# Last two slabs of the output projection taken token tile by token tile, and the first two tiles of the norm before the channel mixer turned by transposes

## What is computed

```python
mix = jnp.concatenate([h_ml.reshape(B, T, ML_WIDTH), h_cm.reshape(B, T, CM_WIDTH)], axis=-1)
x = x + gt1 * (mix @ w_out)
h2 = rmsnorm(x, g_norm2) * (1 + sc2) + sh2
a, bb = jnp.split(h2 @ w_gate_up, 2, axis=-1)
x = x + gt2 * ((jax.nn.silu(a) * bb) @ w_down)
```

## Time and profile of the kernel before

| | us |
|---|---|
| median of 3 executions | 2568.75 |
| lowest, highest | 2564.78, 2570.92 |
| the profiled execution, its own time | 2567.24 |
| its span, first to last instruction | 2565.6 |
| PE busy in it | 2484.3 (97%) |
| DVE busy | 1203.4 (47%) |
| ACT busy | 846.5 (33%) |

### The profile page before, as it was taken

One profiled execution on the slowest core, in us unless ns is written; L12 is line 12 of the kernel. 1 busy time (PEld: TensorE's weight loads), 2 busy tenths in 40 slices (PEclk: granted clock), 3 DMA queues, 4 the chain that ended last, 5 costly groups with the idle time before them and its releaser, 6 DMA issues.

```text
span 2565.6 us, 32860 instructions
## 1 busy us (share of the span) xinstructions
PE 2484.3 (97%) x12360; PEld 1996.8 (78%) x12360; DVE 1203.4 (47%) x1759; ACT 846.5 (33%) x1148; POOL 161.5 (6%) x130
## 2 busy tenths in 40 slices
PE   4999999999999999999999999999989999999997
PEld 2678777788888788888888888888857877777775
DVE  4557544434337554444336554444365754333323
ACT  2243322233244243333244243333244323333211
POOL 0022000000004000000003000000002300000000
PEclk8999999999999999999999999999989999999998
DMA  7732545332342243332242233332333222222222
GB/s 270 247 102 84 173 149 157 92 100 99 99 125 67 94 123 94 94 101 94 89 140 74 95 115 94 95 98 91 103 118 107 79 73 75 82 81 81 85 89 75
DMA packets 358691, 275.93 MB, mean 108 GB/s; under 512 B 10992, under 2 KB 302356, under 8 KB 358567
## 3 DMA queue, kind: packets, MB, share of 16 engines
q1 hardware_dynamic: 330500, 224.57, 29.4%
q10 hardware_dynamic: 24116, 34.95, 4.0%
q0 software_dynamic: 3968, 14.95, 1.5%
HBM read 263.49 MB, written 10.96 MB: 107 GB/s over the span
## 4 chain that ended last, share of the span: by engine, by line
PE 85%; DVE 8%; issue 2%; DMA 2%; ACT 2%; ACTq 1%; POOL 0%; DVEq 0%; POOLq 0%; SPq 0%
PE banks L1751 17%; PE banks L1752 17%; PE banks L1753 17%; PE banks L1804 8%; PE banks L1806 8%; PE banks L1805 8%; PE banks L1765 1%; PE banks L1629 1%; DVE w_lo L1263 1%; DMA raw<-in_w_in_dram 1%; ACT w_hi L784 1%; PE banks L1775 1%; PE banks L1879 1%; DVE hT_lo L1269 1%; DVE x L1591 1%
## 5 line engine op out<-in xcount | busy, mean ns | idle before, releaser
L1751 PE MATMUL banks<-hT_hi,w_lo 128*128 128x512 f32 x2176 | 868.2, 399 | 11.0 <-DVE w_lo L1263 8.5
L1752 PE MATMUL banks<-hT_lo,w_hi 128*128 128x512 f32 x2176 | 853.3, 392 | 0.0
L1753 PE MATMUL banks<-hT_hi,w_hi 128*128 128x512 f32 x2176 | 852.4, 392 | 0.0
L1263 DVE TENSOR_TENSOR w_lo<-raw,w_hi 128x1024 fp32r<-128x1024 f32 x392 | 480.4, 1226 | 646.9 <-ACT w_hi L784 635.7
L784 ACT ACTIVATE w_hi<-raw 128x1024 fp32r<-128x1024 f32 x392 | 412.6, 1053 | 470.8 <-PE banks L1806 442.7
L1751 PEld LDWEIGHTS banks<-hT_hi,w_lo 128*128 128x128 f32 x2176 | 412.1, 189 | 115.9 <-issue 15.5
L1753 PEld LDWEIGHTS banks<-hT_hi,w_hi 128*128 128x128 f32 x2176 | 411.6, 189 | 88.2
L1752 PEld LDWEIGHTS banks<-hT_lo,w_hi 128*128 128x128 f32 x2176 | 412.2, 189 | 81.3
L1804 PE MATMUL banks<-w_lo,act_hi 128*128 128x512 f32 x704 | 277.2, 394 | 0.0
L1806 PE MATMUL banks<-w_hi,act_hi 128*128 128x512 f32 x704 | 274.2, 390 | 0.0
L1805 PE MATMUL banks<-w_hi,act_lo 128*128 128x512 f32 x704 | 274.1, 389 | 0.0
(11 more groups left out here) (332 smaller groups left out, 1880.4 us busy)
## 6 DMA issues: line engine op xcount, KB each, us to landing
raw<-in_w_gate_up_dram SPq DMA_DIRECT2D x176, 512.0 KB, 3.7
raw<-in_w_in_dram SPq DMA_DIRECT2D x96, 512.0 KB, 3.8
raw<-in_w_down_dram SPq DMA_DIRECT2D x88, 512.0 KB, 3.7
ada_stage<-in_w_ada_dram ACTq DMA_DIRECT2D x8, 2048.0 KB
raw<-in_w_out_dram SPq DMA_DIRECT2D x32, 512.0 KB, 3.7
in_stage<-in_w_in_dram ACTq DMA_DIRECT2D x6, 2048.0 KB
stage<-in_w_ada_dram SPq DMA_DIRECT2D x4, 2048.0 KB
x_sb<-in_x_prompt_dram POOLq DMA_DIRECT2D x4, 2048.0 KB, 9.0
```

The costliest lines, as they stand in the source:

```text
L1263: ve.tensor_tensor(w_lo[:, s % 2], raw[:, s % 2], w_hi[:, s % 2].bitcast(F32), ALU.subtract).then_inc(lo_done.sem, 1)
L1751: mm(out, w_lo[:, slot, k, :], rhs_hi[:, r, :], start=start and n == 0, stop=False)
L1752: mm(out, w_hi[:, slot, k, :], rhs_lo[:, r, :], start=False, stop=False)
L1753: ins = mm(out, w_hi[:, slot, k, :], rhs_hi[:, r, :], start=False, stop=stop and last)
```

## The change

The last two output slabs are no longer taken one after the other. When slab 6 is due PE waits for it, skips it, waits for slab 7 as well, and then does for each token tile the six matmuls of slab 6 and the six of slab 7. `out_tiles` on DVE now takes the mean square of a tile directly behind its residual sum, and the factor's use one tile later. For the first two tiles (ROW_TILES = 2) DVE and ACT multiply the rows themselves by the factor into `xn` (left half DVE, right half ACT), and PE turns them with transposes; for tiles 2 and 3 the diagonals stay, now for all eight pieces of a tile in one go. ACT's split of S_UP moves to the point in front of the squares of tile 3; in the last block DVE's copy to `s_ev` moves in front of the mean of tile 3, and the piece whose PSUM bank it frees is turned late.

```diff
+ROW_TILES = 2
@@ ACT
+            def scale_tile_right(blk, i):
+                act.wait_ge(rs.sem, rs.at(blk, i + 1))
+                act.activation(xn[:, KT // 2:KT, i, :], x1[:, i, BLK:D].rearrange("p (k e) -> p k e", e=P),
+                               ACT.Copy, scale=rrt[:, i:i + 1]).then_inc(up_right.sem, 1)
...
-                for n in range(1, N_OUT + 1):
+                for n in range(1, N_OUT):
                     split_hi(blk, S_OUT + n)
...
                 for i in range(TT):
+                    if i == TT - 1:
+                        split_hi(blk, S_UP)
                     act.wait_ge(zadd.sem, zadd.at(blk, TT + i + 1))
                     squares(blk, 0, x1, BLK, D, 1, rows=(i,))
+                    if 0 < i <= ROW_TILES:
+                        scale_tile_right(blk, i - 1)
@@ DVE
+            def scale_tile_left(blk, i):
+                ve.wait_ge(rs.sem, rs.at(blk, i + 1))
+                ve.tensor_scalar(xn[:, 0:KT // 2, i, :], x1[:, i, 0:BLK].rearrange("p (k e) -> p k e", e=P),
+                                 rrt[:, i:i + 1], None, ALU.mult).then_inc(up_left.sem, 1)
...
-                    if j == 1 and i > 0:
-                        tile_mean(blk, TT, i - 1)
-                    if j == 1 and i > 1:
-                        tile_diagonal(blk, i - 2)
+                    if j == 0:
+                        continue
+                    if i > 0:
+                        if i <= ROW_TILES:
+                            scale_tile_left(blk, i - 1)
+                        else:
+                            tile_diagonal(blk, i - 1)
+                    if last and i == TT - 1:
+                        ve.tensor_copy(s_ev[:, :], N2[:, :]).then_inc(sem("s_evict"), 1)
+                    tile_mean(blk, TT, i)
...
-                tile_mean(blk, TT, TT - 1)
-                for i in (TT - 2, TT - 1):
-                    tile_diagonal(blk, i)
-                if last:
-                    ve.tensor_copy(s_ev[:, :], N2[:, :]).then_inc(sem("s_evict"), 1)
+                tile_diagonal(blk, TT - 1)
                 split_lo(blk, S_UP)
@@ PE, up_norm
+                        if i < ROW_TILES:
+                            ins = pe.transpose(out, xn[:, k, i, :], ident[:, :])
+                        else:
+                            ins = mm(out, x1[:, i, k * P:(k + 1) * P], dg[:, i, :], start=True, stop=True)
...
+                held = UP_NORM_BANK.index(N2)
+                left, right = range(KT // 2), [k for k in range(KT // 2, KT) if not last or k != held]
+                for i in range(ROW_TILES):
+                    pe.wait_ge(up_left.sem, up_left.at(blk, i + 1))
+                    turn(i, left)
+                for i in range(ROW_TILES):
+                    pe.wait_ge(up_right.sem, up_right.at(blk, i + 1))
+                    turn(i, right)
+                for i in range(ROW_TILES, TT):
+                    pe.wait_ge(dg_tile.sem, dg_tile.at(blk, i - ROW_TILES + 1))
+                    if last and i == TT - 1:
                         pe.wait_ge(sem("s_evict"), 1)
+                        for r in range(TT - 1):
+                            turn(r, (held,))
+                    turn(i, [*left, *right] if last and i < TT - 1 else range(KT))
@@ PE, output slabs
                     slab_ready(blk, S_OUT + n)
+                    if n == N_OUT - 2:
+                        continue
                     for i in range(TT):
...
+                        if n == N_OUT - 1:
+                            ins = tile_product(OUT_BANK[i][:, :], (n - 1) % 2, mix_hi, mix_lo, 2 * (q - 1), i,
+                                               False, False)
+                            if i == TT - 1:
+                                ins.then_inc(slab_used.sem, 1)
                         ins = tile_product(OUT_BANK[i][:, :], n % 2, mix_hi, mix_lo, 2 * q, i, q == 0,
                                            q == OUT_Q - 1, before_k=ready)
```

More of the change, by code:

```diff
@@ L327, in hybrid_step @@
         MEANS = {-1: 0, 0: TT, 1: TT + 1, 2: TT + 2}
-        dg_tile = signal("dg_tile", TT)
+        dg_tile = signal("dg_tile", TT - ROW_TILES)
+        up_left = signal("up_left", ROW_TILES)
+        up_right = signal("up_right", ROW_TILES)
         left_scaled = signal("left_scaled", TT)
@@ L1403, in tile_ready, with out_tiles @@
                     ve.wait_ge(slab_used.sem, slab_used.at(blk, end))
-            def out_tiles(blk, j):
+            def out_tiles(blk, j, last):
                 cols = slice(j * BLK, (j + 1) * BLK)
@@ L1521, in ve_block @@
                     if n % OUT_Q == 0:
-                        out_tiles(blk, n // OUT_Q - 1)
-                tile_mean(blk, TT, TT - 1)
-                for i in (TT - 2, TT - 1):
-                    tile_diagonal(blk, i)
-                if last:
-                    ve.tensor_copy(s_ev[:, :], N2[:, :]).then_inc(sem("s_evict"), 1)
+                        out_tiles(blk, n // OUT_Q - 1, last)
+                tile_diagonal(blk, TT - 1)
                 split_lo(blk, S_UP)
@@ L1826, in turn @@
                             pe.wait_ge(out_read.sem, out_read.at(blk, TT + {0: 1, 5: 2, 6: 3, 7: 4}[k]))
-                        ins = mm(UP_NORM_BANK[k][:, i * P:(i + 1) * P], x1[:, i, k * P:(k + 1) * P], dg[:, i, :],
-                                 start=True, stop=True)
+                        out = UP_NORM_BANK[k][:, i * P:(i + 1) * P]
+                        if i < ROW_TILES:
+                            ins = pe.transpose(out, xn[:, k, i, :], ident[:, :])
+                        else:
+                            ins = mm(out, x1[:, i, k * P:(k + 1) * P], dg[:, i, :], start=True, stop=True)
                         if i == TT - 1:
                             ins.then_inc(trx.sem, 1)
[L1832 to L1836, removed]
+                held = UP_NORM_BANK.index(N2)
[9 more added lines that the diff above has]
+                    if last and i == TT - 1:
                         pe.wait_ge(sem("s_evict"), 1)
-                    for i in range(TT):
-                        turn(i, (k,))
+                        for r in range(TT - 1):
+                            turn(r, (held,))
+                    turn(i, [*left, *right] if last and i < TT - 1 else range(KT))
             def norm_out(blk, ks):
```

## The result

| | us |
|---|---|
| median of the kernel before | 2566.13 (2562.49 to 2570.92, 6 runs) |
| median of the changed kernel | 2579.51 (2577.84 to 2583.02, 6 runs) |
| ratio after to before, 95% interval | 1.0053 (1.0039 to 1.0066) |
| difference | +13.4 (+10.0 to +16.9) |
| profiled execution of after, its own time | 2578.35 (span 2576.7) |

The change makes the kernel slower by half a per cent. The two differences agree once one sees that the profiled execution of after lies 1.2 under its median, and that of before 1.1 over its median.

What follows compares the result with a forecast made beforehand. PE was busy 97%, held before the up slabs by DVE's chain. 2.57 + 0.11 - 0.58 = 2.10 us per block, 6.3 for three, +0.15 last: +6.4; clock +4.4; +10.8 on 2567.9 gives 2578.7 us, range 2571 to 2586.

Steps and rivals of the forecast that it cites:

- The wait: PE ahead of slab 6: waits for slab 7's split, 2.57 us per block in three blocks, 1.97 in the last.
- The 0.11 of the first matmul: PE's first matmul after the new wait takes 0.50 us instead of 0.39, adding 0.11 per block.
- DVE's backlog: Tiles 2.72 us apart let DVE keep up; tile 3's gate product starts 0.20 after its end, 0.58 us gained per block.
- The margins: DVE's means and ACT's work between tiles fit with 0.2 to 0.3 us to spare, costed at nothing.
- The chain behind tile 3: From tile 3's gate product to the last diagonal: unchanged at 3.22 us.
- The turns: PE's passes behind the last diagonal: 16 instead of 40, 2.8 us less work, costed at nothing because DVE's pieces don't wait.
- the turns were the bound: Rival: passes behind the last diagonal set the end, so a gain of 4.2 us, 2563.7 us; chance 0.06.
- The last block's sum: Last block: 1.97 wait less 0.64 samples' product, 0.58 backlog and 0.60 copy to `s_ev`, +0.15 us.
- The clock: Behind the new wait the granted clock falls in two of three blocks at 2.2 us each, +4.4 us.
- 1.58 us is harmless: PE's clock: an idle stretch of 1.58 us left it at 1.00, whereas one of 3.05 ended below.
- The transposes as a rival: Rival: transposes don't count as work for PE's clock, up to 1.8 us per block more, 2584.0 us; chance 0.10.
- What moved along: SP's slab loads and POOL's load of the next block's rows stay or shift with the chain; nothing gained or lost.

Runs made afterwards that it cites:

- e1: The kernel before with one wait more: PE waits for slab 7's split ahead of slab 6, old order kept; 2579.43 us against 2565.04, ratio 1.0057.
- e3: The changed kernel with slab 7 in a third slot of its own, so PE need not wait for its split; 2565.75 us against 2565.04, ratio 1.0001.
- e6: The changed kernel with slabs 6 and 7 one after the other again; scaled rows, transposes and new DVE/ACT order stay; 2577.6 us against 2565.7, ratio 1.0043.
- e5: The changed kernel with the two middle blocks written out on ACT and DVE instead of looped; one execution, 2574.54 us beside 2565.7.
- e4: The changed kernel with ROW_TILES = 0, all four tiles scaled by diagonals, none turned by transposes; 2579.81 us, ratio 1.006 to before.
- e2: The changed kernel with ten unneeded products (five in the last block) filling PE's wait for slab 7; 2575.09 us, ratio 1.0041 to before.
- e8: The four-slot kernel with early up-slab splits, plus ACT writing the high part of norm pieces 2 and 5; 2560.11 us, ratio 0.9979 to before.
- e10: The changed kernel with slabs 6 and 7 in extra slots and early up-slab splits, run once more; 2557.33 us against 2565.21, ratio 0.9969.
- e7: The changed kernel with slabs 6 and 7 in own slots and the first two up slabs split early, except last block; 2557.51 us against 2565.7, ratio 0.9964.
- e9: The kernel before, old slab order and diagonals, with the extra slots and early splits of the first two up slabs; 2556.32 us against 2565.21, ratio 0.9966.

## Why the prediction was right, and where it wasn't

The forecast (slower, 2578.7) has the right sign and size: 2579.51. That the two lie within 1 us is in part luck. The forecast stood on 2567.9 for before, whose six runs have a median of 2566.13; the difference was forecast at +10.8 and measured at +13.4 (10.0 to 16.9). Step by step it is less tidy, too.

**The wait** (part 1) was read rightly from the split's times: 2.57 forecast, 2.56 to 2.57 in the looped blocks, 2.72 in the first, where it was not read separately. The 0.11 of the first matmul is there too (11.01 against 10.88). Only this step was needed for the sign; e1 shows that it carries the result, and e3 that without it nothing remains.

**DVE's backlog** (part 2), 0.58 forecast, 0.57 and 0.65 measured. The margins held: tile 2's mean ends 0.17 before tile 3's product starts, without holding it up. e6 shows the size of what was costed at nothing: with tiles 1.36 apart the same order puts DVE 3.6 us behind.

**The chain behind tile 3** (part 3) failed as a step in two of the four blocks. "The old one, 3.22" held in the first and the last block (3.14: 0.84, 0.73, 0.75, 0.82). In the second and third it is 3.84: 0.36 more from product to sum and 0.27 more to the squares, of which 0.17 comes back before the first piece. A block costs 2.59 to 2.63 there instead of 2.10; the first block, without its fall, costs 2.15. e5 shows that it goes when the looped blocks are written out; its cause stays open. No row of before showed it, since DVE was behind and busy at that point.

**The turns** at nothing: 9.79 from the first piece to the second up slab, unchanged, and the pieces still 1.064 apart, so "the turns were the bound" is refuted. PE reaches the first up product 2.0 to 2.6 us sooner after slab 7 and doesn't get further by it. But "nothing" was the net of two things that the prediction didn't name. Had the diagonals stayed in this order, the step to the first piece would have cost 1.1 to 1.5 more per block (e4). And in the last block the shorter turns leave PE idle for 1.87 us, where before it went straight on to the samples' product; behind that idle stretch the clock fell in six of the seven kernels that have 1.87 us or more of it (after, e2, e3, e5, e8 and e10, not e7), and at that place in none of the three without it (before, e1, e9). Of the two with 1.44 it held in e4 and fell in e6. In after this costs 1.5, in e2 and e5 3.1. Whether the transposes ahead of the idle stretch have a part in it isn't separated: e4 has none and held, but its stretch is also shorter than the 1.87; e6, with transposes and the same 1.44, fell, but had fallen just before as well.

**The last block's sum** without that fall is -0.08 (34.35 - 32.92 - 1.51); +0.15 was forecast. The copy of `s_ev` left the chain as described: 0.61 for 0.60.

**The clock.** Two falls were forecast at 2.2 us. There were two, one of them at another place than any forecast, at 1.6 and 1.5. So +6.4 and +4.4 became +7.3 and +3.1, and 0.7 came from elsewhere: the sum was right because two errors of about 1 us cancel, and that is luck. The price was the term that was mis-sized: 2.2 was taken from two rows of one trace, 1.5 to 1.6 was measured. Those rows told how long a fall had lasted that once. Behind the same wait of the first block's up slabs (3.05 to 3.33) the slices give 3.1 in before and after, but 1.5 to 1.7 in each of e1 to e6. The number of falls can't be read from the wait: with the same wait it was 1, 3, 3 and 2 in the traces of four kernels. The mean of these, 2.25 of three, is near the two that were taken, but one execution can't tell. And the lower anchor, "1.58 us is harmless", doesn't stand: the same idle stretch of 1.58 in the last block, harmless in before, ended in a fall in e1, the only one of the twelve traces where it did:

```profile
2137.79:2139.37 1.58, 0.00 (x1) 1.00 0.00 0
...
2140.70:2143.70 3.00, 3.00 (x36) 0.51 0.00 0
```

**The transposes as a rival.** In the first three blocks 16 transposes followed by 32 diagonal passes left the clock where it was (in the second block the first up product starts at 907.37, and 907 to 909 is at a granted 1.00). The Trainium skill (TensorE: Matmul & The Clock Gate, Part 4: PE-mode transpose) says that the full clock doesn't engage for transposes, which don't count as busy in the same way. These stretches don't show that. But the rival isn't refuted everywhere: in e6 an idle stretch of 1.73 to 1.84 among the transposes was followed by a fall in all four blocks, while idle stretches of 1.47 (after, e4 and e5) and 1.99 (e1) in front of slab 6 in the last block, with no transposes beside them, held. For e6 and for the last block the question stays open.

**What moved along**, SP's loads, was rightly put at nothing for this change: the wait of 3.1 us among the first block's up slabs is there before and after. But it was the largest thing to be had nearby, as e7 and e9 show, and the prediction passed over it with one sentence.

## What to carry to other kernels

Before two steps are merged into one, look up when the last input of the second is ready: here one slot for two slabs turned the split of slab 7, until then hidden under slab 6, into a wait of PE, 2.6 us in each of three blocks and 2.0 more in the last, and no saving downstream of it was as large. An engine that finishes sooner but whose successor is bound by another engine has only gained idle time, and on TensorE idle time can cost the clock as well: filled with products that nobody needs, the same wait cost 1.6 us less wherever it had brought a fall. And a chain should be followed past its end to the queue that feeds the next stage: the same two splits, done early, moved the loads and took away a wait that lay 11 us behind the second up slab.

## What the runs showed of the hardware that was not expected

- An idle stretch's length alone doesn't decide whether the granted clock falls: 1.58 us left it at 1.00 in before and brought it to 0.51 in e1; 1.44 us held in e4 and not in e6; 1.73 to 1.84 us fell in all four blocks of e6, and 1.99 us held in e1; 1.87 to 1.88 us fell in five kernels and held in e7; 2.40 to 2.56 us fell 9 times of 12.
- The fall can come well after the work has resumed: in the last block of after 1.86 us of work still ran at 0.99, and the 3 us behind them at 0.50. Elsewhere it came at once (after's first block, 0.50 in the 3.20 us behind the wait) or before the end of the idle stretch (a mean of 0.94 over the wait in e1's first block, and of 0.89 over the 3.05 us of the earlier trace rows).
- In the looped blocks of after two neighbouring instructions of DVE, with only a semaphore's signal between them, started 1.19 us apart instead of 0.84, and ACT began 1.08 instead of 0.73 after the instruction that released it; written out, both delays were gone (e5), and in the loop the first was missing in before and e7, the second in e4.
